# Hidden activations of the expert blocks turned by DMA and VectorE instead of TensorE, and GpSimd's gather moved ahead of the previous block's addition and store

## What is computed

```python
xbuf = jnp.zeros((n_rows, d), x.dtype).at[dest].set(x[flat_tok])   # rows sorted by expert, padded to blocks of 128
def expert_block(args):
    xb, e = args                                   # xb: 128 x 1024
    hid = jax.nn.silu(xb @ w1[e]) * (xb @ w3[e])   # 128 x 512
    return hid @ w2[e]                             # 128 x 1024
ybuf = lax.map(expert_block, (xbuf.reshape(n_blocks, EXPERT_BLOCK, d), blk_e))
y = ybuf[dest].reshape(t, TOP_K, d) * gate[..., None]
h = layer_norm(ALPHA * h + jnp.sum(y, axis=1), ln2_g, ln2_b)
```

## Time and profile before

| | |
|---|---|
| median of 3 runs | 1349.43 us (1348.34 to 1349.52) |
| the profiled execution: time, span | 1348.61 us, 1346.7 us |
| TensorE matmul busy | 1311.8 us, 97% of the span |
| VectorE busy | 958.0 us, 71% |
| ScalarE busy | 511.7 us, 38% |
| GpSimd busy | 526.8 us, 39% |
| granted TensorE clock, mean | 0.996 of full |
| chain that ended last | PE 94%, DVE 2%, issue 2%, DMA 1% |

### The profile page before, as it was taken

One profiled execution on the slowest core, in us unless ns is written; L12 is line 12 of the kernel. 1 busy time (PEld: TensorE's weight loads), 2 busy tenths in 40 slices (PEclk: granted clock), 3 DMA queues, 4 the chain that ended last, 5 costly groups with the idle time before them and its releaser, 6 DMA issues.

```text
span 1346.7 us, 20368 instructions
## 1 busy us (share of the span) xinstructions
PE 1311.8 (97%) x6382; PEld 1096.1 (81%) x6383; DVE 958.0 (71%) x1357; ACT 511.7 (38%) x568; POOL 526.8 (39%) x543
## 2 busy tenths in 40 slices
PE   6999999999999999998999999999999999999995
PEld 5888888888888888887888888888888888888884
DVE  7758577687759785698777886665675677776564
ACT  3423234322443234323444454343443454444251
POOL 2001010111101110022566665755665656666555
PEclk9999999999999999999999999999999999999998
DMA  9635534563455344544777774563554545666421
GB/s 276 172 91 162 153 110 157 172 192 106 156 189 157 109 141 164 208 177 174 284 267 252 271 271 146 193 233 135 181 202 182 191 165 211 237 229 238 146 70 64
DMA packets 156522, 243.58 MB, mean 181 GB/s; under 512 B 18944, under 2 KB 84992, under 8 KB 156480
## 3 DMA queue, kind: packets, MB, share of 16 engines
q1 hardware_dynamic: 118624, 154.15, 35.3%
q0 software_dynamic: 28928, 71.74, 15.0%
q10 hardware_dynamic: 8928, 17.13, 3.7%
HBM read 211.97 MB, written 64.62 MB: 205 GB/s over the span
## 4 chain that ended last, share of the span: by engine, by line
PE 94%; DVE 2%; issue 2%; DMA 1%; POOL 1%; ACT 0%; SPq 0%; DVEq 0%; POOLq 0%
PE acc L520 29%; PE acc L522 29%; PE acc L521 28%; PE tp L560 4%; PE logits L599 2%; PE aux L830 1%; DMA b_in<-in_ln_in_b 1%; PE logits L645 0%; DMA xg<-h_scratch,gat_now 0%; DVE xt_lo L1570 0%; DVE ring_lo L1239 0%; PE aux L522 0%; PE aux L520 0%; PE aux L521 0%; PE aux L670 0%
## 5 line engine op out<-in xcount | busy, mean ns | idle before, releaser
L520 PE MATMUL acc<-ring_hi 128*128 128x512 f32 (+1 forms) x800 | 309.0, 386 | 1.8 <-DVE ring_lo L1239 1.6
L522 PE MATMUL acc<-ring_hi,ring_lo 128*128 128x512 f32 (+1 forms) x800 | 305.6, 382 | 0.0
L521 PE MATMUL acc<-ring_lo,ring_hi 128*128 128x512 f32 (+1 forms) x800 | 305.2, 382 | 0.0
L520 PE MATMUL acc<-ring_hi,xt_hi 128*128 128x512 f32 x648 | 256.5, 396 | 4.2 <-issue 2.1
L522 PE MATMUL acc<-ring_hi,xt_lo 128*128 128x512 f32 x648 | 252.7, 390 | 0.0
L521 PE MATMUL acc<-ring_lo,xt_hi 128*128 128x512 f32 x648 | 252.6, 390 | 0.0
L1802 POOL TENSOR_TENSOR small<-small 128x1 f32<-128x1 f32 x31 | 47.4, 1528 | 358.9 <-DVE small L1208 358.9
L520 PEld LDWEIGHTS acc<-ring_hi 128*128 128x128 f32 x800 | 151.3, 189 | 29.9 <-DVE ring_lo L1239 2.4
L522 PEld LDWEIGHTS acc<-ring_hi,ring_lo 128*128 128x128 f32 x800 | 151.1, 189 | 29.1
L521 PEld LDWEIGHTS acc<-ring_lo,ring_hi 128*128 128x128 f32 x800 | 151.4, 189 | 27.8
L921 ACT CAST ring_hi<-stage_x 128x2048 fp32r<-128x2048 f32 x64 | 119.5, 1916 | 76.6 <-PE acc L522 76.0
(11 more groups left out here) (276 smaller groups left out, 1886.4 us busy)
## 6 DMA issues: line engine op xcount, KB each, us to landing
stage_x<-in_exp_w SPq DMA_DIRECT2D x64, 1024.0 KB, 6.4
stage<-in_w_in SPq DMA_DIRECT2D x64, 512.0 KB, 5.4
stage<-in_exp_w SPq DMA_DIRECT2D x32, 1024.0 KB, 6.4
stage<-in_w_out SPq DMA_DIRECT2D x32, 512.0 KB, 5.2
h_scratch<-hres POOLq DMA_DIRECT2D x16, 512.0 KB, 3.0
sum_scratch<-hres ACTq DMA_DIRECT2D x16, 512.0 KB, 3.0
hrow<-in_x POOLq DMA_DIRECT2D x12, 512.0 KB, 4.8
h_scratch<-hrow POOLq DMA_DIRECT2D x12, 512.0 KB, 3.0
```

The costliest lines, as they stand in the source:

```text
L520: nc.tensor.matmul(dst, w_hi, x_hi, start=start, stop=False)
L521: nc.tensor.matmul(dst, w_hi, x_lo, start=False, stop=False)
L522: return nc.tensor.matmul(dst, w_lo, x_hi, start=False, stop=stop)
```

## The change

Blocks 1 to nb-2 no longer have their `hid` transposed on TensorE. After `hid_rows(b)` ScalarE issues a store of `hid` to a scratch tensor in DRAM (`hid_out`: 512 pieces of 512 bytes), waits for it to land, and issues a load of 128 rows of 2 KB back into `hid_q` (`hid_back`); at the start of its next turn VectorE transposes `hid_q` in blocks of 32 x 32 into `aux` (`hid_turn`). The order of the hidden index that results is matched by loading w2 in four quarters of 32 partitions. `silu(b)` goes ahead of `hid_hi(b-1)` on ScalarE. The three or four table entries become one word, so each turn loads one register. On GpSimd the next gather goes ahead of `final_put` of the block before. Block 0 and the last block keep TensorE's transposes, with `hid_rows` written in four parts.

```diff
@@ SyncE: load_expert, w2
-                src = v[ex // NEG, ex % NEG, :, (j % 2) * kts:(j % 2 + 1) * kts, :]
-                sp.dma_start(dst, src).then_inc(s_stage[j], 16)
+                    for a in range(QUARTERS):
+                        src = w2_v[ex // NEG, ex % NEG, a, :, (j % 2) * 2:(j % 2 + 1) * 2, :]
+                        dst = staged(j)[a * SUB:(a + 1) * SUB, 0, :].rearrange("p (k c) -> p k c", k=2)
+                        sp.dma_start(dst, src).then_inc(s_stage[j], 16)
@@ TensorE: the loop
                 down(pe_of)
-                hid_tile(b)
@@ ScalarE
+            def hid_out(b):
+                act.wait_ge(s_hid, b + 1)
+                act.wait_ge(s_hq, b * 16)
+                act.dma_start(hid_by_token, hid[:].rearrange("p (a f) -> p a f", f=P)).then_inc(s_hst, 16)
+            def hid_back(b):
+                act.wait_ge(s_hst, b * 16 + 16)
+                act.dma_start(hid_q[:], hid_dram).then_inc(s_hq, 16)
             def turn(b, first):
-                e_of = act.value_load(table[0:1, 0, bass.ds(b, 1)], min_val=0, max_val=NE - 1)
-                e_next = act.value_load(table[0:1, 0, bass.ds(b + 1, 1)], min_val=0, max_val=NE - 1)
-                ends = act.value_load(table[0:1, 1, bass.ds(b, 1)], min_val=0, max_val=1)
+                word = act.value_load(table[0:1, 1, bass.ds(b, 1)], min_val=0, max_val=4 * NE - 1)
                 if not first:
+                    silu(b)
                     hid_hi(b - 1)
-                    silu(b)
...
                 gate_col(b + 1, e_next)
                 act.wait_ge(s_w3, b + 1)
+                hid_out(b)
                 x_hi(b + 1)
+                hid_back(b)
                 with act.If(ends > 0):
...
                     units_hi(e_of + 1, 1)
@@ VectorE
+            def hid_turn(b):
+                dve.wait_ge(s_hq, b * 16)
+                V.transpose(aux[:].rearrange("p (k r b) -> p k b r", k=FT, r=SUB),
+                            hid_q[:].rearrange("p (b k c) -> p k b c", k=FT, c=SUB)).then_inc(s_hturn, 1)
             def turn(b, first):
...
                 if not first:
-                    if split:
-                        hid_lo(b - 1)
+                    hid_turn(b)
+                    hid_lo(b - 1)
@@ GpSimd
-            def block_end(b, rows):
-                index_put(b)
+            def block_end(b, rows, prev=None):
                 at0 = isinstance(b, int) and b == 0
                 if not at0:
+                    if rows:
+                        index_rows(b + 3)
+                        gather_rows(b + 3)
+                    final_put(prev, prev + 1)
+                index_put(b)
+                if not at0:
                     index_sums(b + 1)
...
-                final_put(b, b + 1 if rows else b + 2, None if rows else b + 1)
```

More of the change, by code:

```diff
@@ L1571, in x_lo, with hid_rows @@
                                     ALU.subtract).then_inc(s_xtlo, 1)
-            def hid_rows(b):
+            def hid_rows(b, by_tile=False):
                 dve.wait_ge(s_silu, b + 1)
                 dve.wait_ge(s_w3, b + 1)
-                if not (isinstance(b, int) and b == 0):
-                    dve.wait_ge(s_htr, b)
+                if isinstance(b, int) and b == 1:
+                    dve.wait_ge(s_htr, 1)
+                elif not (isinstance(b, int) and b == 0):
+                    dve.wait_ge(s_hst, b * 16)
                 dve.wait_ge(s_gcol, b + 1)
                 col = gate_0 if isinstance(b, int) and b == 0 else gate[:, bass.ds(b, 1)]
-                V.scalar_tensor_tensor(out=hid[:], in0=act_a[:], scalar=col, in1=acc[1][:], op0=ALU.mult,
-                                       op1=ALU.mult).then_inc(s_hid, 1)
+                if by_tile:
+                    tiles = hid[:].rearrange("p (k a c) -> p a k c", k=FT, c=SUB)
+                    parts = [(tiles[:, a], *(t[:, a * P:(a + 1) * P].rearrange("p (k c) -> p k c", c=SUB)
+                                             for t in (act_a, acc[1]))) for a in range(QUARTERS)]
+                else:
+                    parts = [(hid[:], act_a[:], acc[1][:])]
+                for to, x_a, x_b in parts:
+                    ins = V.scalar_tensor_tensor(out=to, in0=x_a, scalar=col, in1=x_b, op0=ALU.mult, op1=ALU.mult)
+                ins.then_inc(s_hid, 1)
+            def hid_turn(b):
+                dve.wait_ge(s_hq, b * 16)
+                V.transpose(aux[:].rearrange("p (k r b) -> p k b r", k=FT, r=SUB),
+                            hid_q[:].rearrange("p (b k c) -> p k b c", k=FT, c=SUB)).then_inc(s_hturn, 1)
             def hid_lo(b):
@@ L1750, in _ @@
             dve.wait_ge(s_elo[2], 2)
+            dve.sem_inc(s_hturn, 1)
             turn(1, True)
             nb1 = dve.value_load(nblocks[0:1, 1:2], min_val=NE, max_val=NB - 1)
-            turn(2, False, split=False)
-            with dve.Fori(3, nb1) as b:
+            with dve.Fori(2, nb1) as b:
                 turn(b, False)
@@ L1986, in block_end @@
                     gather_sums(b + 1)
[L1988 removed]
+                else:
+                    final_put(b, b + 2, b + 1)
             def last_end(b):
```

76 lines of the change are left out of this document (47 added, 29 removed).

## The result

The changed kernel takes **1491.88 us** (median of 4 runs, 1490.33 to 1492.7); the kernel before took 1349.47 (4 runs, 1348.34 to 1352.06) in the same comparison. The ratio is 1.1046, with a 95% interval of 1.1032 to 1.1059: 142 us slower. The forecast was 1385 us with a range of 1335 to 1415. Its direction was right, its size was a quarter of the loss.

A forecast was written before the change was run, and what follows sets the result against it. TensorE, busy 97% of the span, was taken as the bound. Transposes save 17.1 us, 15 changing turns add waits: 15 L - 9.5 = +35.5 at L = 3.0, so 1385 us, range 1335 to 1415.

The forecast's parts named there:

- L: Time from issue to landing of ScalarE's new store of hid; taken as 3.0 us, with 2.2 below and 5.3 above.
- changing turns: Turns in which the next expert's weights are cast; 15 counted, eight priced as three-block and seven as two-block.
- 15 L - 9.5: Whole-kernel sum, 8 (L - 0.8) + 7 (L + 2.0) - 17.1; +35.5 us at L = 3.0.
- the term of the middle turns: Store, load and transposition in turns without weights, taken as covered by slack and costed at nothing.
- the chain behind the landing: Load issue, w3 casts and subtractions, sums, transposition, `ht_lo` before `down`; TensorE waits L - 0.8 us in three-block changing turns.
- Both transfers are back before VectorE's next turn: In turns without weights, store and load finish within the slack, so the round trip there costs nothing.
- TensorE's saving of 0.45 a block: Four transposes leave TensorE's path in each of 38 blocks, 17.1 us in all; iterations go from 17.7 to 17.2.
- the transposition: VectorE's new 128 x 512 transposition of hid; taken as 0.7 us, between 0.59 and twice 0.7.
- the lateness of `xt_lo` in two-block turns: In changing turns of two-block experts TensorE waits 2.2 us for `xt_lo`, against 0.46 before.
- the per-expert form of the sum: A changing turn costs L - 0.8 us for three-block experts, L + 2.0 for two-block; 0.45 saved per block.
- 2.2 in each of six turns: GpSimd's addition no longer collides with VectorE's w1 subtractions (4.49 instead of 6.69 us); this gain is in the sum.
- the store is slow: Rival: 512 small pieces among 2 MB of weight packets, L 5.3 or more, 1419 us and up; chance 0.1.

The follow-up runs named there:

- e2_rows_2k: Changed kernel with the store of hid as 128 rows of 2 KB instead of 512 pieces of 512 bytes; 1464.7 us, measured once.
- e2_quarter: Changed kernel storing only a quarter of hid (64 KB in 128 pieces of 512 bytes) from block 2 on; 1458.9 us, measured once.
- e7_half_w1: Changed kernel loading only half of every w1 unit from expert 2 on (1 MB instead of 2 MB ahead of the store); 1456.3 us, measured once.
- e3_hold_loads: Changed kernel with SyncE's next w1 loads held until the changing turn's store has landed; 1442.29 us, ratio 1.0663.
- e9: Changed kernel with TensorE's transposes, single w2 loads and GpSimd's old order put back; word table and silu's new place kept; 1349.46 us, ratio 0.9995.
- e4: Changed kernel with TensorE's transposes and single w2 loads put back, the rest kept, GpSimd's new order included; 1346.74 us, ratio 0.9971.
- e8: Changed kernel with w3 casts ahead of the landing wait, x casts ahead of the store, and w1, w2, w3 loads held for store landings; 1381.01 us, ratio 1.0225.
- e1: Changed kernel with ScalarE's casts of w3 moved ahead of the wait for the store's landing; 1409.4 us, ratio 1.0419.

## Why the prediction was wrong

- **The step that failed is L**, the landing of the store. I took 3.0 us, from stores of 512 KB "issued while weights load", with 5.3 as the upper end. Over the 15 changing turns it is 9.2 in the mean (137.3 in sum). The formula stands well: 15 L - 9.5 gives +128 with that L, against 142 measured, and most of the rest is the term of the middle turns, below. What I knew and did not weigh is in my own sentence: the store goes out 1 to 3 us after 2 MB of loads. The rows that I took as nearest, of the program's first part, don't stand behind 2 MB. The page of before had a row for what does, the weight loads of 1 MB, with the median us to landing at its end:

```profile
stage<-in_exp_w SPq DMA_DIRECT2D x32, 1024.0 KB, 6.4
```

Two of them, issued just before the store, were to land 6.4 us after their issue; a store behind them could not be expected at 3.0. The estimate by the Trainium skill's page "DMA: Bandwidth & Descriptors", section "Anatomy of one DMA" (2.6 us for 256 KB alone), is near the quiet landings of 2.3, though the page gives its fit for transfers that GpSimd issues and this one was ScalarE's. It has no term for bytes already under way.
- **The clock was not in the sum.** Long waits were followed by matmuls at half clock; 43.5 us in all. Waits of the length that I forecast brought it in some places only: of six of 2.7 us after the change, three were followed by it (702.70, 749.71, 1307.78) and three not (796.83, 844.07, 1260.95). It isn't added to the formula, since while TensorE runs slowly VectorE catches up: in nine of the 14 changing turns with a wait of 4.6 us or more, TensorE still had to wait for `ht_lo` afterwards, 7.5 us in all.
- **The place of the wait** was wrong. I compared the chain behind the landing with `down`; the subtraction of w3 has an earlier customer, the second `up` of the next iteration, 5.5 us behind its start. Most of the wait fell there: 85.3 us, against 9.6 for `ht_lo`.
- **"Both transfers are back before VectorE's next turn"**, which put the middle turns at nothing, failed in the eight behind w2's loads: landing 9.7, then 2.7 for the load, and VectorE waits 19.3 us for `hid_q`. Such a turn took 21.0 us from `hid` to `hid` against 18.9 before. With this term added, the forecast's formula meets every kernel that has ScalarE's casts of w3 behind the landing, within some 6 us; landings and waits are each run's own, in us:

| | 15 landings | waits for `hid_q` | sum - 9.5 | measured loss |
|---|---|---|---|---|
| after | 137.3 | 19.3 | 147.1 | 142.4 |
| e2_rows_2k | 114.0 | 15.1 | 119.6 | 114.1 |
| e2_quarter | 106.7 | 11.4 | 108.6 | 108.3 |
| e7_half_w1 | 97.9 | 19.5 | 107.9 | 106.1 |
| e3_hold_loads | 75.2 | 19.9 | 85.6 | 91.7 |

- **Right:** TensorE's saving of 0.45 a block and iterations of 17.0 to 17.2 without weights; 0.73 for the transposition (I took 0.7; the estimate of 1.24, worked out from the bf16 price in the Trainium skill's page "VectorE: DVE Perf Modes", section "The three transpose paths", is too high for this float32 form); the lateness of `xt_lo` in two-block turns, 2.7 measured against 2.2; the per-expert form of the sum (two blocks: L + 2.0 - 0.9 = 10.7 at L = 9.6, measured 47.0 - 35.9 = 11.1); that the sign turns at an L far below any landing. Four DMAs per w2 unit were never tried by themselves; the register loads and `silu`'s new place gave nothing together (e9).
- **GpSimd:** the reorder gives about 3 us by the medians, but not by the mechanism that I described, since e9 has the old order without long w1 subtractions. I booked 2.2 in each of six turns on VectorE's path; TensorE could get at most the 0.46 that it had lost in each.
- The rival "the store is slow" (1419 and up, chance 0.1) was the true case, mainly for another reason than its own: the bytes ahead, with a smaller part for the form.

Left open: whether a split into both ways (DMA for experts of three blocks, TensorE for those of two) beats e4. By the table it would save 1.4 us in each of eight experts, an estimate; it wasn't tried. Nor were w2's casts ahead of `hid_back`, which by the rows of e8 could start them up to 7 us earlier in an expert of two blocks, an estimate too.

## What to carry to other kernels

Before a round trip through DRAM is put on a critical path, list what other queues issue in the microseconds before it: in this kernel each landing was 2 to 3 us plus roughly the time of the bytes ahead of it, and issuing it from another engine's queue didn't let it pass. That holds for the load back as for the store. Look at what stands behind an engine's wait for such a landing in its order, in every kind of turn: here first the casts of w3, then those of w2. If the wait can't be moved, give the transfer a place in the schedule of the bulk loads, and reckon that holding these moves the heap ahead of the next one. And count that TensorE may run at half clock for a while behind a wait; here that was 1.3 to 3.0 us behind each wait of 4.6 us or more.

## What the runs showed of the hardware

- A store of 256 KB issued by ScalarE landed after 2.3 us alone, 4.6 behind GpSimd's gather of 512 KB, 5.8 behind 1 MB and 8.9 behind 2 MB that SyncE had issued 1 to 3 us earlier; in the last case none of its packets moved for 3.5 us. A quarter of the store's bytes changed a loaded landing only to 6.5 to 8.6. A load of 256 KB took 2.7 us, and 5.6 to 7.2 behind 2 MB (e1).
- After an idle stretch of 5.5 us TensorE's granted clock read 0.50 for 6 us (matmuls 0.43 us apart, from 0.23), then 1.00 again; after three waits of 2.7 us it read 0.50 for 3.4 us, after three others 1.00 throughout, and after 1.14 us (969.04) 1.00.
- GpSimd's addition of 128 x 1024 (2.40 us at 698.67 of e9) beside VectorE's two subtractions of 128 x 2048: before, the two took 6.69 instead of 4.49, and the addition 2.77; in e9 they took 4.48, and the addition 4.49.
- VectorE's transposition of 128 x 512 float32 in 32 x 32 blocks into a bank took 0.73 us, where a plain pass over that size (`ht_lo`) takes 0.69.
